# One core, a two-block model: gates and bias reads in another order, modulation sums by column halves, compression in four column groups

## What is computed

```python
# first block: the modulation, 2 x 9 x 1024 numbers, of which every sublayer takes a shift, a scale and a gate
mods = silu(c) @ ada_w + ada_b

# mixer_ab: gates of the linear attention, and dilated attention with a bias from the distance
bi = p[..., AB_BI:AB_BF] + gate_b[:B_HEADS]
bf = p[..., AB_BF:AB_PROJ] + gate_b[B_HEADS:]
ya = dilated_attention(aq, ak, av, rel_bias)
yb = sigmoid(bo) * head_norm(mlstm(bq, bk, bv, bi, bf), head_g)   # uses cumsum(log_sigmoid(bf))

# mixer_c: blocks of 32 tokens of keys and of values are compressed to one each (15 blocks, 2 groups)
def compress(t, pos, w1, w2):
    blocks = t[:, cidx] + pos[None, None, :, None, :]
    flat = blocks.transpose(0, 3, 1, 2, 4).reshape(Bn, G, n_cmp, CMP_BLOCK * E)   # 32 * 128 long
    return gelu(flat @ w1) @ w2                                                    # w1: 4096 x 256
```

## Time and profile before

| | us |
|---|---|
| median of 3 runs | 2578.42 |
| lowest, highest | 2578.35, 2588.62 |
| the profiled execution, its time | 2581.79 |
| the profiled execution, its span | 2580.0 |
| PE busy in the span | 2429.1 (94%) |
| DVE busy | 1709.2 (66%) |
| ACT busy | 1101.5 (43%) |

### The profile page before, as it was taken

How to read it: one execution, slowest core, us unless ns; L and a number is a source line. 1 busy time by engine, 2 the same in 40 slices (tenths; PEclk the granted TensorE clock), 3 DMA queues, 4 the chain that set the end, 5 groups by cost and what they waited for, 6 DMA issues and landing times.

```text
span 2580.0 us, 40749 instructions
## 1 busy us (share of the span) xinstructions
PE 2429.1 (94%) x17382; PEld 2136.8 (83%) x17382; DVE 1709.2 (66%) x2365; ACT 1101.5 (43%) x1375; POOL 81.4 (3%) x116
## 2 busy tenths in 40 slices
PE   3999989999999998889999989999999989999998
PEld 3999748999999777779999868788888858788886
DVE  5987566876886455655555665548895375557985
ACT  2333254334333033433334443447774252546773
POOL 0000000000000003630000000000000000000000
PEclk9999989999999998889999978999999989999999
DMA  7887304774876230004554503549984400747991
GB/s 294 326 312 270 123 25 158 288 282 154 310 285 256 98 123 26 3 2 185 201 194 124 180 26 126 227 171 354 367 324 185 169 35 21 290 188 304 368 362 49
DMA packets 48284, 502.10 MB, mean 195 GB/s; under 512 B 4968, under 2 KB 9448, under 8 KB 10856
## 3 DMA queue, kind: packets, MB, share of 16 engines
q1 hardware_dynamic: 42480, 490.52, 50.2%
q10 hardware_dynamic: 5624, 8.97, 1.4%
HBM read 496.33 MB, written 3.15 MB: 194 GB/s over the span
## 4 chain that ended last, share of the span: by engine, by line
PE 82%; DVE 11%; ACT 3%; DMA 2%; issue 2%; POOL 1%; ACTq 0%; DVEq 0%; POOLq 0%
PE PS L1229 25%; PE PS L585 25%; PE PS L655 7%; PE PS L631 4%; PE PS L548 2%; DMA ring<-stream 1%; PE PS L668 1%; PE PS L1323 1%; PE PS L568 1%; DVE work L1879 1%; DMA xT<-x_in 1%; PE PS L964 1%; PE PS L767 1%; PE PS L1280 1%; DVE w_up_lo L1915 1%
## 5 line engine op out<-in xcount | busy, mean ns | idle before, releaser
L585 PE MATMUL PS<-x_part_hi,w_up_hi 128*128 128x256 f32 x1408 | 404.4, 287 | 9.4 <-DVE x_part_lo L1950 6.5
L585 PE MATMUL PS<-x_part_lo,w_up_hi 128*128 128x256 f32 x1408 | 399.4, 284 | 0.0
L585 PE MATMUL PS<-x_part_hi,w_up_lo 128*128 128x256 f32 x1408 | 399.3, 284 | 0.0
L2489 DVE TENSOR_TENSOR ring_low<-ring,m_w_up 128x2048 fp32r<-128x2048 f32 x128 | 293.1, 2291 | 134.0 <-ACT m_w_up L1727 134.0
L1727 ACT ACTIVATE m_w_up<-ring 128x2048 fp32r<-128x2048 f32 x128 | 245.3, 1917 | 187.5 <-PE PS L1229 187.5
L585 PEld LDWEIGHTS PS<-x_part_hi,w_up_hi 128*128 128x128 f32 x1408 | 271.0, 193 | 12.7 <-issue 8.0
L585 PEld LDWEIGHTS PS<-x_part_lo,w_up_hi 128*128 128x128 f32 x1408 | 271.3, 193 | 0.0
L585 PEld LDWEIGHTS PS<-x_part_hi,w_up_lo 128*128 128x128 f32 x1408 | 271.1, 193 | 0.0
L1229 PE MATMUL PS<-m_w_up,xg_hi 128*128 128x512 f32 x640 | 253.0, 395 | 3.8 <-DVE work L2503 3.8
L1229 PE MATMUL PS<-ring_low,xg_hi 128*128 128x512 f32 x640 | 254.2, 397 | 0.0
L1229 PE MATMUL PS<-m_w_up,xg_lo 128*128 128x512 f32 x640 | 253.2, 396 | 0.0
(11 more groups left out here) (523 smaller groups left out, 5158.8 us busy)
## 6 DMA issues: line engine op xcount, KB each, us to landing
ring<-stream SPq DMA_DIRECT2D x133, 2048.0 KB, 7.8
ring<-stream SPq DMA_DIRECT2D x88, 1536.0 KB, 6.7
work<-stream SPq DMA_DIRECT2D x48, 1024.0 KB, 8.3
hT<-stream SPq DMA_DIRECT2D x16, 1024.0 KB, 7.5
ring<-stream SPq DMA_DIRECT2D x3, 1152.0 KB, 5.6
const<-const_tables ACTq DMA_DIRECT2D x1, 2336.5 KB, 18.7
bias_scratch<-work ACTq DMA_DIRECT2D x1, 2048.0 KB
work<-bias_scratch ACTq DMA_DIRECT2D x2, 1024.0 KB, 7.5
```

Of the source, the lines that this page charges most:

```text
L585: last = mm(out, w[a][:, lo:lo + P], x[b][:, at:at + T], start=start and i == 0, stop=stop and i == 2, skip_group_check=skip)
L2489: tt_(ring_low[n][:, part], ring[n][:, part], m_w_up[g % 3][:, :].bitcast(F32), ALU.subtract).then_inc(S("up_split"), 1)
```

## The change

Four edits. First, `ada_sum` makes two matmuls of 64 columns where it made one of 128; the two write partitions 0 to 63 and 64 to 127. Second, in ab the step on the gates moves ahead of DVE's step 5 and of the first half of the convolution; `load_bias` moves ahead on ACT by six instructions and one copy; the mask is added, and step 14 made, ahead of the last part of the linear attention, and step 15 moves into the attention. Third, the 64 matmuls of the compression write four groups of 32 partitions in turn (32 stationary columns, the last two of which belong to the next blocks), ACT copies 128x256, and the transposes become matmuls with a folding matrix (`C_FOLD`, four small copies on DVE) that adds up the four groups and drops the two extra columns. Fourth, ACT's step 11 of c moves from between the two copies to behind the gelu.

```diff
@@ ada_sum, PE @@
                 for m in range(4):
-                    last = mm(bank(b + p % 2, 4)[:, m:m + 1], z[:, m * P:(m + 1) * P], ones[:, 0:1], start=True,
-                              stop=True)
+                    for lo in (0, 64):
+                        last = mm(bank(b + p % 2, 4, 0, lo, lo + 64)[:, m:m + 1], z[:, m * P + lo:m * P + lo + 64],
+                                  ones[:, 0:1], start=True, stop=True)
@@ c, PE @@
                         for i in range(16):
-                            last = mm(bank(4 + 2 * kv, T, T, 0, 2 * NCMP), b3[:, 16 * half + i, :],
-                                      piece(name)[:, i * T:(i + 1) * T], start=(half == 0 and i == 0),
-                                      stop=(half == 1 and i == 15))
+                            at, lo = 2 * NCMP * (16 * half + i), 32 * (i % 4)
+                            n = 32 if at + 32 <= 960 else 2 * NCMP
+                            last = mm(bank(4 + 2 * kv, T, T, lo, lo + n), b3[:, at:at + n],
+                                      piece(name)[:, i * T:(i + 1) * T], start=(half == 0 and i < 4),
+                                      stop=(half == 1 and i >= 12), skip_group_check=True)
...
-                        last = nc.tensor.transpose(bank(4 + 2 * kv + m, 2 * NCMP),
-                                                   W(C_RAW + kv * T + m * P, P, 0, 2 * NCMP),
-                                                   ident[0:2 * NCMP, 0:2 * NCMP])
+                        last = mm(bank(4 + 2 * kv + m, 2 * NCMP), W(C_RAW + kv * T + m * P, P), W(C_FOLD, 2 * NCMP),
+                                  start=True, stop=True)
@@ ab, ACT @@
                 mix_highs("ab", 10, 11)
+                act.wait_ge(S("bias_stored"), 16)
+                load_bias(A_BM)
                 copied(0, W(A_Q, 1024), 6)
...
                 copied(1, W(A_K, 1024), 0)
-                act.wait_ge(S("bias_stored"), 16)
-                load_bias(A_BM)
@@ c, ACT @@
-                    fn(W(C_RAW + kv * T, T, 0, 2 * NCMP), bank(4 + 2 * kv, T, T, 0, 2 * NCMP),
-                       ACT.Copy).then_inc(S("cmp_raw"), 1)
+                    fn(W(C_RAW + kv * T, T), bank(4 + 2 * kv, T, T), ACT.Copy).then_inc(S("cmp_raw"), 1)
                     if kv == 0:
-                        mix_highs("c", 10, 11)
+                        mix_highs("c", 10)
...
                 last.then_inc(S("hid_gelu"), 1)
+                mix_highs("c", 11)
@@ ab, DVE @@
-                dve.wait_ge(S("ab_copied"), 1)
-                mix_lows("ab", 4, 5)
-                conv(0, 4)
+                mix_lows("ab", 4)
                 line.next("softlog_ready")
...
                 done(tt_(lf, lf, sl[:, :, 4:8], ALU.subtract), "lin_fed")
+                mix_lows("ab", 5)
+                dve.wait_ge(S("ab_copied"), 1)
+                conv(0, 4)
...
                 hh = ls(4352, 1024)
+                dve.wait_ge(S("bias_in"), 32)
+                bm = W(A_BM, 8 * ATT).rearrange("p (h c) -> p h c", c=ATT)
+                done(tt_(bm, bm, C("dilated").unsqueeze(1).broadcast_to([P, 8, ATT]), ALU.add))
+                mix_lows("ab", 14)
                 line.next("lnum_copied")
...
-                mix_lows("ab", 14, 15)
-                dve.wait_ge(S("bias_in"), 32)
-                bm = W(A_BM, 8 * ATT).rearrange("p (h c) -> p h c", c=ATT)
-                done(tt_(bm, bm, C("dilated").unsqueeze(1).broadcast_to([P, 8, ATT]), ALU.add))
-                attention("ab", {4: [linear_out], 5: [lambda: mix_lows("ab", 16)], 6: [linear_low]})
+                attention("ab", {4: [linear_out], 5: [lambda: mix_lows("ab", 16)], 6: [linear_low], 2: [lambda: mix_lows("ab", 15)]})
@@ c, DVE @@
+                for lo in range(0, P, 32):
+                    last = v.tensor_copy(W(C_FOLD, 2 * NCMP, lo, lo + 32), ident[lo:lo + 32, lo:lo + 2 * NCMP])
                 done(last, "cmpb_ready")
```

More of the change, by code:

```diff
@@ L319, in build @@
         C_SRC, C_RAW = 4096, 14528
+        C_FOLD = 10400
         C_ATT = 18432
@@ L1317, in c @@
                 for kv in range(2):
-                    b3 = W(C_CMPB + 960 * kv, 960).rearrange("p (i n) -> p i n", n=2 * NCMP)
+                    b3 = W(C_CMPB + 960 * kv, 960)
                     for half in range(2):
```

## The result

The changed kernel took 2551.9 us (median of four, 2541.9 to 2554.0) where the kernel before took 2578.7 in the same session: a ratio of 0.9879, interval 0.9843 to 0.9915. The forecast was 2551, so direction, size and nearly all places were right. One term, the sums, was too small by half, and ab brought 0.4 to 3 us more than its 14.0. The ratios are not quite those of the medians: the medians differ by 26.8 and 37.9 us, the ratios make it 31 us (22 to 40) and 37 us (32 to 42), and these overlap.

A forecast was written before the change was run, and what follows sets the result against it. PE holds 82% of the chain of waits, DVE 11%. Terms -2.9 - 7.7 - 6.3 - 10.8 = -27.7 took the profiled 2581.8 to 2554.1, less 3.4 for the median: 2551 us, range 2538 to 2564.

The forecast's parts named there:

- Sums, -2.9: Modulation sums by column halves: about 0.09 us saved on each of 32 in PE's stream, -2.9 us, bounds 0 and -10.
- The switch of the tiling mode: Around each halved sum, changing the array's shape costs 0.09 us ahead and again behind, before any exposed weight load.
- The gates, -7.7: In ab, moving `lf` ahead removes PE's 5.4 us wait and 2.3 us of lower clock: -7.7, bounds -5.4 and -8.2.
- Ahead of the attention, -6.3: In ab, mask and step 14 fill DVE's idle 4.33 us, step 15 goes into the attention: -6.3 us, bounds -4 and -11.
- late bias: Rival in ab: bias reads share queues with ab_out.1 and DVE waits; 6.6 us are lost, 2557; chance 0.08.
- Phase c, -10.8: Compression in four column groups, its end set by loads, c_out.0 releasing ACT's step 10: -10.8 us, bounds -6 and -13.
- 7 and 14: Bounds in us for the compression's 128 records in column groups, which took 29.30; 7 is four groups at once.
- Halves one after another: Rival on the sums: column halves load in turn, each sum costs 0.34 us more, +11 us, 2565; chance alone 0.05.
- nothing in c: Rival: four column groups bring nothing in the compression, so c's -10.8 becomes +1, 2563; chance alone 0.05.
- The first rival: Another name for "Halves one after another": a sum's 16 records take 0.88 us, +11 in place of -3; chance alone 0.05.
- Falls of the clock at the sums: Rival: the granted clock falls at every sum, 32 x 2.3 = 72 us added, 2623; chance 0.03.
- The clock coming back in both attentions: Rival: ab's attention runs at full clock, bounded by DVE, and c's gains a little too, 2545; chance 0.13.

The follow-up runs named there:

- e9_nosums: The changed kernel with the modulation sums undone (eight records of 128 columns again): 2552.1 us, ratio 0.9881 to the kernel before.
- e2_gates: The kernel before with only DVE's `lf` step on the gates moved ahead of step 5 and the convolution: 2572.8 us, ratio 0.9972.
- e3_ab: The kernel before with all of the change's ab edits (gates, bias read, mask, steps 14 and 15): 2568.7 us, ratio 0.9959.
- e5_after: The changed kernel, unchanged, run again in a second session: 2545.4 us, ratio 0.9858 to the kernel before.
- e6_two: The changed kernel with the compression in two column groups of 64 in place of four of 32: 2553.1 us, ratio 0.9888 to the kernel before.
- e7_free10: The changed kernel with c's step 10 on ACT behind the gelu and step 11 inside the attention: 2542.8 us, ratio 0.9848 to the kernel before.
- e1: The kernel before with only the modulation sums split into two column halves: 2577.0 us, ratio 0.998.
- e4: The kernel before with only c's edits: compression in four column groups, the fold, step 11 behind the gelu; 2569.1 us, ratio 0.9955.
- e10_quarters: The changed kernel with each modulation sum in four column groups of 32 in place of two of 64: 2542.5 us, ratio 0.9849 to the kernel before.

## Why the prediction was right, and where not

- **The base.** The profiled execution before was 3.4 us above its median, and the prediction took that off. The other traces show where it may lie: in mla's attention, which no part of the change touches, e9_nosums is 4.0 us ahead of before. The windows of before and of e9_nosums from 300 to 383 us show the granted clock at 0.86 and 0.90:

```profile
300.00:383.00 83.00, 73.25 (x273) 41.97 (x271) 47.28 (x91) 35.68 (x80) 0.00 (x0) 0.86 0.17 64
```

```profile
300.00:383.00 83.00, 74.58 (x291) 42.39 (x290) 51.04 (x104) 38.31 (x90) 0.00 (x0) 0.90 0.18 64
```

- **Sums, -2.9: the mechanism right, the size too small.** Measured are -4.5 in the ffn phases (32 times the median of 0.14) and -1.4 to -1.8 at the head. The prediction had 0.32 from the records less 0.23 for the switches and loads. The first is 0.26 (0.70 less 0.44 from the first record's start to the last's), the second only 0.12: 0.09 on the way in, as the row of rwkv had it, and 0.03 on the way out, for which I had taken as much again and an exposed load. And "I count nothing" for the four ahead of ffn0 fails: a sum took 1.86 us there and takes 1.02, and two of the four are waited for by DVE. The last one, before and after (timeline of PE):

```profile
41.52 1.86 PE L568 MATMUL PS<-const,work 128*128 128x1 f32 x8 [4.34 <-DVE work L1879]
```

```profile
40.59 1.02 PE L570 MATMUL PS<-const,work 128*64 128x1 f32 x16 [5.19 <-DVE work L1882]
```

- **The switch of the tiling mode.** On the way in it costs 0.09 us; on the way out the next matmul starts only 0.015 us later than behind a whole sum (0.127 in place of 0.112), and the one behind it 0.02 later. The Trainium skill (TensorEngine Tiling (Array Packing), Key Properties) says that a change of the mode drains the array; the trace agrees on the way in.
- **The gates, -7.7: right.** -8.2 by the trace of e2_gates, -7.2 by its times. No wait of PE at L1092, and 11.34 us for the 96 matmuls.
- **Ahead of the attention, -6.3: right.** From ab_in.5's end to the first scores it is 7.0 us less in e3_ab, after and e5_after; 0 to 1 us of it is given back in the attention (28.0 us in place of 27.5 in the profile after, +0.5 for a forecast of +0.3). Of "late bias" nothing is seen. I expected the bias reads near 1462, in the time of day of before; with the 10.1 us by which ab begins earlier they stand at 1456.8, and 16 us of cover were 19.
- **Phase c, -10.8: right**, -9.5 to -11.4 up to the attention, and for the reason given. On before's time (add the 29.6 us by which c begins earlier) step 10 begins at 2056.2 where the prediction put 2057, and DVE's attention (2035.19 after) at 2064.7, predicted 2065.3. One term came out by luck. From the second copy to DVE's attention it was 5.4 us before, the prediction added 1.0 for step 11, and 6.7 were measured (2028.45 to 2035.19). But step 11 isn't in the chain. What is longer there are PE's products with cmp_w2, 1.03 and 1.83 us in place of 0.60 and 0.99: the granted clock is 0.50 there, as this window of after has it, and was 1.00 before:

```profile
2024.00:2034.00 10.00, 4.97 (x24) 3.80 (x20) 3.88 (x2) 6.10 (x10) 0.00 (x0) 0.50 0.63 265
```

  The prediction had no term for a lower clock ahead of c's attention; it fell at about 2021.8, just behind PE's wait of 2.45 us for cmp_w1.3. At full clock the compression's records take 0.054 us each, 6.9 for all 128, which is the lower bound of "7 and 14"; the first 96 took 6.7 us because the clock was 0.50 for the first 3.4. e6_two, at full clock 0.108 each and so at the upper bound, costs at most 2.2 us more in the stage, which shows that PE isn't the bound, and e7_free10 that c_out.0 is.
- **The rivals.** Halves one after another, nothing in c and the late bias are shown wrong, by e1, e4 and the rows above. The first rival's own sum is off by a little: 0.88 less 0.81 and the 0.23 make 0.30 a sum, not 0.34, so +10 us and not +11. Falls of the clock at the sums: they didn't come; the windows 54 to 311, 377 to 837 and 1149 to 1400 us of after, in which the 32 sums lie, all have a granted clock of 1.00. The clock coming back in both attentions: it did not. It was 0.63 in ab's attention (0.54 before) and 0.80 in c's (0.84 before).
- **The sum.** By the stages, sums 6.2, ab 15 to 17 and c 10.4 make -32 to -33, five more than the forecast. Two thirds of the five are the sums. That 2551 lies within 1 us of the first session's median is therefore luck: the ratios, -31 and -37 with the stages' -32 to -33 between them, say that the terms together were some five too small. That the medians of the two sessions are 11 us apart (-26.8 and -37.9) shows no difference of the kernel, which was the same: stretches of lower clock in untouched stages come to as much (+5 and +5 in and behind c in the kernels above). Why they fall where they do in one execution and not in another, no run here tells; and whether the three slower executions of the first session had them is not shown, since only the quickest was profiled.
- **Better ones.** e7_free10 and e10_quarters are each quicker than the changed kernel in the stage that they touch (-3 and, by its rows, -6.3), and their ratios to before, 0.9848 and 0.9849, stand 0.001 below its 0.9858. Both beat the kernel before clearly; their margin over the changed one, some 2.5 us, is within the error. The two together were not run.

## What to carry to other kernels

Before pricing a faster piece of engine work, follow the loads behind it in the ring: four column groups took some 20 us out of PE's time in c, and the end moved by half of it, since a transfer, issued when an earlier piece is used up, released a step of ACT that stood between two copies. A step that waits for a transfer doesn't belong between two copies on the chain. And compare kernels stage by stage, at the same instruction: a single profile of this kernel carries 5 to 10 us of clock from stages that nobody changed.

## What the runs showed of the hardware

- Column groups that share all 128 rows load and multiply beside each other: one-column sums take 0.70 us whole, 0.44 in halves, 0.26 in quarters (8, 16 and 32 records; first to last start), and a matmul of 256 columns takes 0.217 us alone and 0.054 in four groups. The Trainium skill (TensorE: Matmul & The Clock Gate, What overlaps and what doesn't) says that a weight load passes a running matmul only in another row group. The trace disagrees, by this reckoning: 128 columns of weights take 0.10 us from record to record, so 32 columns one behind another would take 0.025 (an estimate), and in quarters a record follows at 0.011.
- The profile's clock column can't be trusted at the start of the program. A whole sum took 1.86 us there and one in halves 1.02, in place of 0.95 and 0.63 amid the ffn matmuls, and the plain float32 matmuls of 256 columns right behind it (L548) start 0.427 us apart until 47.6 and 0.216 apart from then on, the two paces that the compression's records of 256 columns have in e1_sums at 0.50 and at 1.00. The column reads 1.00 for both; the trace's first record of the clock is at 47.6. Two windows of before:

```profile
44.30:47.30 3.00, 3.00 (x9) 2.37 (x8) 0.00 (x0) 0.00 (x0) 0.00 (x0) 1.00 0.94 393
48.00:51.00 3.00, 3.00 (x16) 2.64 (x15) 1.08 (x1) 1.66 (x2) 0.00 (x0) 1.00 0.02 8
```

  So the sums ahead of ffn0 ran at the lower of the two levels, and the edit earned 0.84 us on each of the last two there (ahead of which PE had stood still for DVE for 4 to 5 us), against 0.14 in the stream.
- With 30 matmuls added at the places where PE had stood still, the granted clock was 1.00 for 27 us up to and into the attention (0.51 from 2028 to 2052 without them), and it fell 6 us into the attention, over which it was 0.82.
